# Two layers on one core: norm and residual stretches by token halves, two product blocks on either side computed half by half around them, squares stationary in their sums

## The reference

```python
mix = jnp.einsum('bld,de->ble', merged, w_out)
x = x + rmsnorm(mix, g_post_mix)
h = rmsnorm(x, g_pre_mlp)
ff = jnp.einsum('blf,fd->bld', jnp.square(jax.nn.relu(jnp.einsum('bld,df->blf', h, w_ff1))), w_ff2)
return x + rmsnorm(ff, g_post_mlp)
```

## Time and profile before

| | us |
|---|---|
| median of 3 runs | 3941.4 |
| lowest, highest | 3940.68, 3949.42 |
| profiled execution, its own time | 3946.39 |
| its span | 3944.7 |
| TensorE, busy | 3585.1 (91%) |
| VectorE (DVE) | 1385.7 (35%) |
| ScalarE (ACT) | 955.5 (24%) |
| GpSimd (POOL) | 979.0 (25%) |

### The profile page before, as it was taken

The page is one execution under the profiler, slowest core; times in us unless marked ns, Lnnn a source line. Parts: engine busy times, 40 slices in busy tenths (PEclk is TensorE's granted clock), DMA queues, the critical chain, the costliest instruction groups (busy, mean ns, idle before and its releaser), DMA issues.

```text
span 3944.7 us, 43154 instructions
## 1 busy us (share of the span) xinstructions
PE 3585.1 (91%) x16432; PEld 2868.9 (73%) x16432; DVE 1385.7 (35%) x1430; ACT 955.5 (24%) x1074; POOL 979.0 (25%) x469
## 2 busy tenths in 40 slices
PE   7988999896998999999888979899869899999995
PEld 5766887785875888888667867676657578888884
DVE  6713665443315221312223436352334332121122
ACT  3112235443112111111212333332321221011111
POOL 1101111111333222222331115051125322222224
PEclk9988999998998999999898999899989899999997
DMA  3334343324412111111233221112254311111113
GB/s 111 91 63 161 109 151 107 107 70 155 144 59 97 53 43 53 43 48 48 82 102 108 94 81 65 70 65 95 88 186 155 97 58 48 48 46 49 43 48 122
DMA packets 107205, 341.55 MB, mean 87 GB/s; under 512 B 15488, under 2 KB 25600, under 8 KB 107024
## 3 DMA queue, kind: packets, MB, share of 16 engines
q1 hardware_dynamic: 105600, 335.02, 25.7%
q10 hardware_dynamic: 1472, 4.72, 0.3%
HBM read 252.99 MB, written 86.57 MB: 86 GB/s over the span
## 4 chain that ended last, share of the span: by engine, by line
issue 42%; PE 33%; POOL 10%; DVE 7%; DMA 3%; ACT 3%; POOLq 0%; SPq 0%; ACTq 0%; DVEq 0%
PE pair L302 25%; POOL w_lo L267 6%; PE bank L626 2%; POOL hg_sc L1233 2%; PE bank L504 1%; PE wide L663 1%; DVE act_lo L410 1%; PE wide L400 1%; DVE p L472 1%; DVE foxr L637 1%; ACT w_hi L265 0%; DVE s_tmp L749 0%; DMA act_hi<-mixed 0%; PE wide L368 0%; DMA f2x<-x 0%
## 5 line engine op out<-in xcount | busy, mean ns | idle before, releaser
L267 POOL TENSOR_TENSOR w_lo<-w_raw,w_hi 128x1024 fp32r<-128x1024 f32 x276 | 676.3, 2451 | 2529.2 <-ACT w_hi L265 2528.9
L302 PE MATMUL pair<-act_hi,w_hi 128*128 128x512 f32 x3184 | 1050.9, 411 | 26.6 <-POOL w_lo L267 21.3
L302 PE MATMUL pair<-act_lo,w_hi 128*128 128x512 f32 x3184 | 1009.7, 398 | 0.0
L302 PE MATMUL pair<-act_hi,w_lo 128*128 128x512 f32 x3184 | 1007.5, 397 | 0.0
L302 PEld LDWEIGHTS pair<-act_hi,w_hi 128*128 128x128 f32 x3184 | 586.6, 191 | 181.2 <-issue 34.8
L302 PEld LDWEIGHTS pair<-act_lo,w_hi 128*128 128x128 f32 x3184 | 604.8, 190 | 148.5
L302 PEld LDWEIGHTS pair<-act_hi,w_lo 128*128 128x128 f32 x3184 | 602.8, 189 | 148.3
L265 ACT CAST w_hi<-w_raw 128x1024 fp32r<-128x1024 f32 x276 | 287.6, 1043 | 608.9 <-PE pair L302 574.5
L472 DVE TENSOR_TENSOR p<-pair,rs 128x1024 f32<-128x1024 f32 x103 | 125.7, 1222 | 492.3 <-PE pair L302 473.6
L1504 DVE TENSOR_TENSOR f2v<-pair,rs 128x1024 f32<-128x1024 f32 x44 | 53.9, 1225 | 356.9 <-PE pair L302 354.1
L302 PE MATMUL pair<-f1hh,w_hi 128*128 128x512 f32 x512 | 157.6, 389 | 0.0
(11 more groups left out here) (424 smaller groups left out, 3860.2 us busy)
## 6 DMA issues: line engine op xcount, KB each, us to landing
w_raw<-in_stream SPq DMA_DIRECT2D x278, 512.0 KB, 3.5
proj<-p SPq DMA_DIRECT2D x103, 512.0 KB, 2.6
m2g<-proj SPq DMA_DIRECT2D x36, 512.0 KB, 4.4
m1g<-proj SPq DMA_DIRECT2D x27, 512.0 KB, 3.3
foxx<-proj SPq DMA_DIRECT2D x32, 256.0 KB, 5.2
act_hi<-mixed SPq DMA_DIRECT2D x16, 512.0 KB, 4.2
n1x<-in_x ACTq DMA_DIRECT2D x8, 512.0 KB, 8.3
fx_cb<-fox_cum SPq DMA_DIRECT2D x8, 512.0 KB, 6.5
```

Of the source, the lines that this page charges most:

```text
L267: nc.gpsimd.tensor_tensor(wlo[:, slot, :], raw[:, slot, :], whi[:, slot, :].bitcast(F32), ALU.subtract).then_inc(s_split, 1)
L302: last = nc.tensor.matmul(out_pair[:, h * HALF:(h + 1) * HALF], wt, a[:, h * HALF:(h + 1) * HALF], start=k == 0 and n_pass == 0, stop=k == ...
```

## The change

`bridge` takes over the last two blocks of the product before it (`tail`) and the first two of the one after it (`head`), both as `TwoBlocks`, whose tiles can be asked for by block o, token half h and tile k; both weight units stay in their slots for all of it, so a unit is released later. Everything in between is done for the first 512 tokens and then for the second. The sums for the next norm are made with the squares as weights and one column of ones moving (`half_sums`), and no longer with ones as weights. x is fetched whole ahead of time, into `hl` or `act_lo`, which are free then; the sum replaces `y` and is stored from there once both halves are there. The first layer's x is read from a copy, `x0`, made in DRAM before `fox`. The barriers at both ends of the bridge are gone; behind f1 there is one. The buffers of a layer's `mix_out` and `mlp` are shared (`Late`), and the first turn of the stage behind a bridge is left out, as before. All buffers of x, scale and squares are reused ones.

```diff
+    x0, x1, x2, x3 = (scratch(n, (KT, P, L)) for n in ("x0", "x1", "x2", "x3"))
...
-    class Ahead:
-
-
-
-        def __init__(self, turns):
-            self.turns = turns
-            self.tiles = products(0, used["units"], 2, 2, KT, act_rhs, lambda *a: self.evict(*a))
-
-        def tile(self, mark):
-
-            PE.after(mark)
-            next(self.tiles)
-
-        def run(self, evict, per):
-            self.evict = evict
-            for _ in self.tiles:
-                pass
-            advance(2, 2)
-            stage(self.turns - 1, 2, 2, KT, act_rhs, lambda i, *a: evict(i + 1, *a), per=per)
...
+    class TwoBlocks:
+        def __init__(self, tiles, rhs):
+            self.tiles, self.rhs = tiles, rhs
+            self.base, self.begun = used["units"], False
+            self.pairs = [(used["blocks"] + o) % 2 for o in range(2)]
+            self.ready = {}
+            advance(2, 2)
+        def tile(self, o, h, k):
+            b = self.base + o
+            slot, half = b % 2, slice(h * HALF, (h + 1) * HALF)
+            reads, out = pair_read[self.pairs[o]], pair[self.pairs[o]][:, half]
+            if not self.begun:
+                self.begun = True
+                split_unit(b + 1, 1 - slot, (b + 1) // 2 + 1)
+                fetch_unit(b + 3, 1 - slot)
+            if k == 0 and h == 0:
+                nc.tensor.wait_ge(s_split, b + 3)
+                nc.tensor.wait_ge(reads.sem, reads.n)
+            hi, lo = self.rhs(o, k)
+            w_hi, w_lo = (x[:, slot, k * P:(k + 1) * P] for x in (whi, wlo))
+            for n_pass, (wt, a) in enumerate(((w_hi, hi), (w_hi, lo), (w_lo, hi))):
+                last = nc.tensor.matmul(out, wt, a[:, half], start=k == 0 and n_pass == 0,
+                                        stop=k == self.tiles - 1 and n_pass == 2)
+            if k == self.tiles - 1:
+                if h == 0:
+                    self.ready[o, h] = PE.mark(last)
+                else:
+                    last.then_inc(s_mm, 1)
+                    self.ready[o, h] = (s_mm, b + 3)
+                    if o == 0:
+                        split_unit(b + 2, slot, b // 2 + 2)
+                        fetch_unit(b + 4, slot)
+        def evicted(self, o, h, evict):
+            at = self.pairs[o]
+            evict(o, slice(h * HALF, (h + 1) * HALF), pair[at][:, h * HALF:(h + 1) * HALF], self.ready[o, h],
+                  pair_read[at].mark)
+    def half_sums(ps, sq, start, stop, mark):
+        PE.after(mark)
+        for j in range(4):
+            last = nc.tensor.matmul(ps[:, j:j + 1], sq[:, j * P:(j + 1) * P], ones[:, 0:1],
+                                    start=start and j == 0, stop=stop and j == 3)
+        return PE.mark(last)
+    def half_root(n, ps, scale, mark):
+        tk = tok[:, 4 * n:4 * n + 4]
+        V.mark(V.after(mark).tensor_scalar(tk, ps[:, 0:4], scale, EPS, ALU.mult, ALU.add))
+        return A.mark(A.after(V.last()).activation(tk, tk, ACT.Sqrt))
+    def half_spread(n, ps, root, dst):
+        tk = tok[:, 4 * n:4 * n + 4]
+        PE.after(V.mark(V.after(root).reciprocal(tk, tk)))
+        for j in range(4):
+            last = nc.tensor.matmul(ps[:, j * P:(j + 1) * P], tk[:, j:j + 1].to_broadcast([P, P]), ident[:],
+                                    start=True, stop=True)
+        return A.mark(A.after(PE.mark(last)).copy(dst, ps))
+    def bridge(tail, tail_evict, y, squares, x, x_ready, r, sq, gain, out_dram, next_gain, head=None, head_evict=None):
+        halves = [slice(h * HALF, (h + 1) * HALF) for h in range(2)]
+        sides = [wide[:, half] for half in halves]
+        last = tail.tiles - 1
+        for o in range(2):
+            for k in range(tail.tiles):
+                tail.tile(o, 0, k)
+            tail.evicted(o, 0, tail_evict)
+        summed = G.last()
+        for k in range(5):
+            tail.tile(0, 1, k)
+        root = half_root(0, bank[0][:], 1.0 / D, half_sums(bank[0][:], squares[:, halves[0]], True, True, summed))
+        for k in range(5, tail.tiles):
+            tail.tile(0, 1, k)
+        tail.evicted(0, 1, tail_evict)
+        for k in range(2):
+            tail.tile(1, 1, k)
+        y_scale = [half_spread(0, bank[0][:], root, r[:, halves[0]]), None]
+        for k in range(2, tail.tiles):
+            tail.tile(1, 1, k)
+        scaled, added, split, done = {}, {}, {}, {0: [], 1: []}
+        def scale(h, k):
+            scaled[h, k] = V.mark(V.after(y_scale[h]).scalar_tensor_tensor(
+                y[:, k, halves[h]], y[:, k, halves[h]], col(gain, k), r[:, halves[h]], ALU.mult, ALU.mult))
+        def step(h, k):
+            yk, half = y[:, k, halves[h]], halves[h]
+            if k < KT - 1:
+                scale(h, k + 1)
+            lane = G if k > 1 else V
+            added[h, k] = lane.mark(lane.after(scaled[h, k], x_ready[k]).tensor_tensor(yk, yk, x(k)[:, half], ALU.add))
+            if h:
+                SP.wait_ge(*added[0, k])
+                SP.wait_ge(*added[1, k])
+                stores[k % 2].mark(SP.dma_start(out_dram[k], y[:, k, :]))
+            if not next_gain:
+                return
+            g = col(next_gain, k)
+            a = A.mark(A.after(added[h, k]).activation(act_hi[:, k, half], yk, ACT.Copy, scale=g))
+            split[h, k] = V.mark(V.after(a).scalar_tensor_tensor(act_lo[:, k, half], yk, g,
+                                                                 act_hi[:, k, half].bitcast(F32),
+                                                                 ALU.mult, ALU.subtract))
+            free = (done[h][k - 2],) if k > 1 else (done[0][-1], summed) if h else ()
+            a = A.mark(A.after(*free).activation(sq(h, k % 2), yk, ACT.Square))
+            PE.after(split[h, k])
+            head.tile(0, h, k)
+            if k >= lag[h]:
+                head.tile(1, h, k - lag[h])
+            done[h].append(half_sums(sides[h], sq(h, k % 2), k == 0, k == KT - 1, a))
+        lag = (2, 4)
+        scale(0, 0)
+        for k in range(KT):
+            step(0, k)
+            if k == 0:
+                tail.evicted(1, 1, tail_evict)
+                summed = G.last()
+            if k == 2:
+                root = half_root(1, bank[1][:], 1.0 / D, half_sums(bank[1][:], squares[:, halves[1]], True, True, summed))
+            if k == 4:
+                y_scale[1] = half_spread(1, bank[1][:], root, r[:, halves[1]])
+        if next_gain:
+            for k in range(KT - lag[0], KT):
+                head.tile(1, 0, k)
+            root = half_root(2, sides[0], 1.0 / D, done[0][-1])
+        scale(1, 0)
+        for k in range(KT):
+            step(1, k)
+            if next_gain and k == 1:
+                rs_ready = half_spread(2, sides[0], root, rs[:, halves[0]])
+            if next_gain and k in (2, 3):
+                V.after(rs_ready)
+                head.evicted(k - 2, 0, head_evict)
+        if next_gain:
+            root = half_root(3, sides[1], 1.0 / D, done[1][-1])
+            for k in range(KT - lag[1], KT):
+                head.tile(1, 1, k)
+            V.after(half_spread(3, sides[1], root, rs[:, halves[1]]))
+            for o in range(2):
+                head.evicted(o, 1, head_evict)
...
+        def square_row(self, h, n):
+            return (self.x[:, 0, 0:HALF], self.x[:, 0, HALF:L], self.sq[:, 0:HALF])[h + n]
+    def mix_out(late, x_dram, gain, out_dram, next_gain, head_evict):
+        y, sq, squares = late.y, late.sq, late.squares
+        G.mark(G.then().memset(squares[:], 0.0))
+        merged = V.last()
+        nc.tensor.wait_ge(V.sem, V.n - 2)
+        x_ready = [x_in_sem[k].mark(SP.dma_start(late.hl[:, k, :].bitcast(F32), x_dram[k])) for k in range(KT)]
+        def rhs(o, k):
+            if o == 0 and k == KT - 1:
+                PE.after(merged)
+            return act_rhs(o, k)
+        def evict(i, o, psum, ready, read):
+            dst = y[:, bass.ds(i * 2 + o, 1), :].rearrange("p a n -> p (a n)")
+            square_sum(dst, sq[:], squares[:], read(V.after(ready).tensor_copy(dst, psum[:])))
+        def tail_evict(o, half, psum, ready, read):
+            dst = y[:, 6 + o, half]
+            square_sum(dst, sq[:, half], squares[:, half], read(V.after(ready).tensor_copy(dst, psum)))
+        stage(3, 2, 2, KT, rhs, evict, per={A: 2, G: 2})
...
+        bridge(TwoBlocks(KT, act_rhs), tail_evict, y, squares, lambda k: late.hl[:, k, :].bitcast(F32), x_ready,
+               late.scale_row(), late.square_row, gain, out_dram, next_gain, TwoBlocks(KT, act_rhs), head_evict)
...
+        def relu2(o, half, psum, ready, read):
+            a = read(V.then(ready).tensor_tensor(x[:, o, half], psum, rs[:, half], ALU.mult))
+            v = V.mark(V.after(a).scalar_tensor_tensor(x[:, o, half], x[:, o, half], 0.0, x[:, o, half],
+                                                       ALU.max, ALU.mult))
+            done(hh[:, o, half], hl[:, o, half], x[:, o, half], v)
...
+        V.after(*(s.last() for s in stores))
```

(25 more changed lines are left out.)

183 lines of the change are left out of this document (73 added, 110 removed).

## The result

| us | before | after |
|---|---|---|
| median (lowest to highest) of 6 runs each | 3942.8 (3938.7 to 3949.4) | 3966.2 (3963.9 to 3980.8) |
| ratio of after to before, 95% interval | | 1.0064 (1.0047 to 1.0081) |
| span of the profiled execution | 3944.7 | 3962.1 |
| tail's last two blocks until the next stage, o1 / f1 / o2 | 98.4 / 98.4 / 97.8 | 104.4 / 108.8 / 107.4 |

The change costs 0.6% where 0.3% of gain was forecast, and 3966 lies above the range, above rival B's 3958 too. The view by stretches of the kernel after, with the columns of the earlier trace rows. The first three rows are o1's tail, loop and end; then f1's loop and end, and o2's loop.

A forecast was written before the change was run, and what follows sets the result against it. The elementwise part was taken to go at the sum of DVE and POOL, not TensorE. Gains 1.8 + 2.9 + 1.8 + 14 = 20.5 us, minus 9, give 11.5: 3934.9 profiled, median 3930, range 3893 to 3958.

The forecast's parts named there:

- rival B: Slower: TensorE's clock falls inside the loop; at 0.6 the 18 us cost 12 in three stretches: 3958 us, chance 0.13.
- those 18 us: TensorE work per stretch counted in the waits and at the end; at clock 0.85 3.2 us more, 2.5 taken.
- a mean clock under 0.75: Sign that the prediction is wrong: TensorE's mean granted clock in these stages under 0.75 (or at 1.0).
- Tail: Last two blocks of the product before, by halves: first scale ready at about 20.9 us instead of 37.4.
- The sums: Row sums of one half, 4 small products on TensorE: 1.0 us taken at full clock, 1.8 at half clock.
- The waits (1) to (4): In-order waits: after step 2, 3.6 us; after step 4, 2.9; between halves, 5.0; after second half's step 1, 2.0.
- The end: From the last split to the next stage: 7.6 us, where the old kernel took 19.7 after the last split.
- Behind f1: After the first layer's MLP stretch, TensorE waits 6.3 us for late constants and weight split, 3.3 before.
- f2: Stretch after the second layer's last MLP group: scale at 16.4 us, no TensorE steps in its loop, 14 us gain taken.
- x0: DRAM copy of x ahead of fox's loads: fox starts 8 to 13 us later, 9 taken; 17 by the skill's figure.
- The sum: Whole kernel: gains 1.8 + 2.9 + 1.8 + 14 = 20.5 us, minus 9 for the x copy: 11.5.
- Rival C: Waits filled: some 12 of the 14.9 us of waits go in each of three stretches: 3894 us, chance 0.22.

The follow-up runs named there:

- filled: The changed kernel with 64 extra 128x128 matmuls, results unused, in each of three stretches ahead of TensorE's waits: 3943.97 us, ratio to before 1.0009.
- 18 fillers: The changed kernel with the late waits plus 18 extra matmuls in each of three stretches, ahead of the first two steps' tiles: 3921.47 us, ratio to before 0.9939.
- the late waits: The changed kernel with roots, scale copies and hidden evictions that wait for TensorE issued one or two steps later: 3915.76 us, ratio to before 0.9934.
- the kernel with everything moved: The late waits kernel with weight splits on DVE, x copy later, constants behind the stage: 3914.43 us; with its tile at 1 KB 3892.19.

## Why the prediction was wrong

The step that failed is "At 0.85 those 18 us cost 3.2 more; some of it is late anyway: I take 2.5". Rival B, at 0.13, named the mechanism, and its place; I argued it away by the old loop's pace between short waits. But the change itself makes the long ones: TensorE stands 1.53 us ahead of the first step and 3.94 ahead of the second, and 0.4 us into the second wait its clock halves; from then on its sums and tiles, at 1.70 us instead of 0.95 for the sums, feed the waits of DVE and ACT, and those keep it idle. The sign that the prediction had named for being wrong, a mean clock under 0.75, came: 0.63 to 0.67. The three loops took 73.0, 70.7 and 72.4 us, and 66.8, 58.3 and 65.5 once filled: 6.2, 12.5 and 6.9 us each, where 2.5 was taken for loop and end together. With their ends and tails the filled stretches took 285.3 us; the prediction's own sum for them is 285.7 (96.6, 92.5, 96.6). That near agreement is partly luck, since the terms below are off both ways. What made up the rest is below.

- **Tail.** The scale came at 23 us (24.5 in o2, where the clock was 0.93), not 20.9: I let the second block's weights be ready after half a block, 5.6 us, while POOL has the square add ahead of their split. 1.9 to 2.1 us in o1, f1 and o2, 3.4 in f2. No part of the working asked for it.
- **The sums**: 0.95 us at full clock (1.0 taken), 1.70 at half.
- **The waits (1) to (4)**: right in place and order, and in their sum at full clock (14.0 against 13.5), less so one by one. At full clock, in the filled kernel's f1, 3.44, 4.06, 3.12 and 3.35 against 3.6, 4.9 less 2.0, 5.0 with the restart, 2.0 forecast. The last split came 73 us behind the first scale (65 forecast; filled, 66.8 at 0.90).
- **The end**: 8.4 us in o1 at full clock (7.6), 10.5 in o2. In f1 15.4: TensorE was 10.2 us behind DVE at the last root.
- **Behind f1**: 6.94 us of wait for the weights, 6.3 forecast. That it drops the clock for the blocks behind was not in it.
- **f2**: 14.7 (14), by two errors that cancel. The scale came at 19.9, not 16.4. But the part behind it was shorter than the sum of DVE and POOL gave: a scale and an add take turns at 1.67 us, where 0.665 and 1.27, so 1.94, were added. The second half's last adds on POOL, four times 1.67 and a last 1.25:

```profile
3950.73 7.92 POOL L500 TENSOR_TENSOR f2y<-f2y,act_lo 128x512 f32<-128x512 f32 x5 [0.63 <-DVE f2y L492]
```

- **x0**: 10.7 (9), within the bounds of 8 to 13. By the figure of the Trainium skill (SBUF — State Buffer, "A bandwidth-pool intuition that's wrong (but worth ruling out)"; quoted in the prediction) it would have been 17; the measurement is nearer to the rows. While the copy was under way, the queues moved 421 GB/s, more than the 358 of that figure, and a copy's bytes are counted once, though they are both read from and written to DRAM:

```profile
350.00:355.00 5.00, 0.00 (x0) 0.00 (x0) 0.00 (x0) 0.00 (x0) 0.00 (x0) 0.50 1.26 421
```

- **The sum**: o1, f1 and o2 lost 26.0 us where 9.5 of gain stood in the sum (1.8, 5.9, 1.8), 35.5 off; the wait behind f1, f2 and x0 add 1.6, and 8.2 came back in unchanged stretches. That is the 29 us between the forecast for the profiled execution, 3934.9, and its 3963.9. The other 7 between 3930 and 3966 are how each profiled execution stands to its median.
- Rival C (waits filled, 3894) was a statement on the same waits: moved one or two steps, with no operation added or left out, they give 50 us, through shorter waits and a higher clock together.

Open: how a given idle time leads to a drop. The same 3.4 us wait in f2's tail cost the clock in seven kernels and not in two; in after, a wait of 1.9 us in the tail was followed by a drop in o2 (0.65 from 3116 to 3120) and by none in o1; and 18 fillers moved a drop where 64 nearly removed it. How much of the 50 us of the late waits is order and how much is clock is open too. Also, with no edit there, the time between f1 and o2 differs between the kernels by up to 11 us, so what an edit is worth is read from its own stretch, and not from the total alone.

## What to carry to other kernels

When TensorE becomes part of a dependent chain, price the chain at both clocks, and let the range reach the lower one if the chain makes TensorE wait inside it (here 1.5 and 3.9 us stood where the clock fell); a term of 18 us at stake is 18 us of range, in each stretch. Before halving work to overlap it, list each small operation that waits for another engine and issue it one or two steps after its input is due: here that order was worth 50 us and turned the same change from 0.6% slower into 0.7% faster. After adding any tile, compare the mean time of matmuls in code that was not edited.

## What the runs showed of the hardware

- A tile of 128 bytes, used by nothing, slows matmuls whose moving operands lie behind it from 389 to 395 ns and the kernel before by 19.7 us; with one of 1 KB, in the kernel with everything moved, they stay at 389.
- Extra work can shorten a chain: 64 matmuls per stretch, results unused, took 22 us off.
- Two forms of the same sums, 0.95 and 1.02 us at full clock, left TensorE at a clock of 0.67 and 0.88 in the same loop. The loop with the lower clock is the one with more busy time on TensorE (54.8 against 46.1 us), in part because the same matmuls last longer at half clock, so the busy share of a row does not tell the clock.
